# A two-layer hybrid decoder trunk: cross attention by token tile, first transfers reordered, DVE's low halves placed between evacuations, norms by Newton steps on DVE

## What is computed

```python
for l in range(2):
    h = rmsnorm(x, norm_mix[l])
    qa, ka, va, qb, kb, vb, qi, ki, wi, qc, kc, vc, g = split(h @ w_in[l])   # 5316 columns
    # three mixers: stick-breaking attention; top-64 sparse attention; sliding window attention
    merged = gates[0] * (o_a @ w_pa[l]) + gates[1] * (o_b @ w_pb[l]) + gates[2] * (o_c @ w_pc[l])
    x = x + merged @ w_out[l]
    # cross attention, 4 heads of 128, into 256 memory tokens
    q = rmsnorm(rmsnorm(x, norm_x[l]) @ w_xq[l], qn_x[l])
    k, v = split(rmsnorm(mem, norm_mem[l]) @ w_xkv[l]); k = rmsnorm(k, kn_x[l])
    x = x + softmax(q k^T / sqrt(128)) v @ w_xo[l]
    hf = rmsnorm(x, norm_ffn[l])
    x = x + (swiglu(hf) if l == 0 else top-2-of-8 expert swiglu(hf))
```

## Time and profile before

| | |
|---|---|
| median of 3 runs | 1813.37 us (1812.16 to 1819.61) |
| the profiled execution | 1814.6 us, span 1813.0 us |
| PE busy in the span | 95% |
| DVE, ACT, POOL busy | 78%, 61%, 5% |
| mean granted TensorE clock | 0.984 of full speed |

### The profile page before, as it was taken

The page is one execution under the profiler, slowest core; times in us unless marked ns, Lnnn a source line. Parts: engine busy times, 40 slices in busy tenths (PEclk is TensorE's granted clock), DMA queues, the critical chain, the costliest instruction groups (busy, mean ns, idle before and its releaser), DMA issues.

```text
span 1813.0 us, 22257 instructions
## 1 busy us (share of the span) xinstructions
PE 1717.1 (95%) x7776; PEld 1373.4 (76%) x7776; DVE 1405.6 (78%) x1258; ACT 1112.3 (61%) x1006; POOL 93.7 (5%) x68
## 2 busy tenths in 40 slices
PE   6999887999989998879999989999999999999999
PEld 5877666788768676667888878888788888788776
DVE  5798675554477967748888878888888888888897
ACT  4646354444345453537777777777777777877765
POOL 1200000000003000010000000000000000000440
PEclk9999998999999999979999999999999999999999
DMA  8533592555445325409999989999999999999985
GB/s 288 206 107 135 189 349 93 186 184 185 162 140 204 134 104 186 186 22 397 365 361 380 366 314 387 364 380 368 346 390 362 369 387 366 367 362 366 402 328 203
DMA packets 73791, 498.13 MB, mean 275 GB/s; under 512 B 8192, under 2 KB 8960, under 8 KB 17552
## 3 DMA queue, kind: packets, MB, share of 16 engines
q1 hardware_dynamic: 66000, 466.55, 67.9%
q0 software_dynamic: 7328, 29.87, 4.6%
q10 hardware_dynamic: 416, 1.08, 0.2%
HBM read 481.73 MB, written 15.73 MB: 274 GB/s over the span
## 4 chain that ended last, share of the span: by engine, by line
PE 77%; DVE 11%; ACT 4%; issue 3%; DVEq 3%; DMA 2%; ACTq 0%; SPq 0%; POOLq 0%
PE ps L516 24%; PE ps L520 24%; PE ps L512 24%; DVE w_lo L397 3%; DVE w_lo L901 1%; ACT w_hi L392 1%; PE ps L701 1%; DMA raw<-in_layer_tiles 1%; PE ps L1201 1%; DVE hT_lo L505 1%; DVE st L1447 1%; ACT w_hi L831 1%; DVEq L1450 1%; ACT scratch L1366 0%; DMA z<-rows_of_experts 0%
## 5 line engine op out<-in xcount | busy, mean ns | idle before, releaser
L512 PE MATMUL ps<-w_hi,hT_hi 128*128 128x512 f32 (+1 forms) x1552 | 436.5, 404 | 33.6 <-ACT hT_hi L500 10.6
L901 DVE TENSOR_TENSOR w_lo<-raw,w_hi 128x2048 fp32r<-128x2048 f32 x168 | 391.3, 2331 | 64.2 <-ACT w_hi L831 64.2
L901 DVE TENSOR_TENSOR w_lo<-z,w_hi 128x2048 fp32r<-128x2048 f32 x168 | 386.6, 2305 | 57.1 <-ACT w_hi L831 56.1
L516 PE MATMUL ps<-w_hi,hT_lo 128*128 128x512 f32 (+1 forms) x1552 | 424.3, 396 | 0.8 <-DVE hT_lo L505 0.4
L520 PE MATMUL ps<-w_lo,hT_hi 128*128 128x512 f32 (+1 forms) x1552 | 422.2, 394 | 0.7 <-DVE w_lo L397 0.7
L512 PEld LDWEIGHTS ps<-w_hi,hT_hi 128*128 128x128 f32 x1552 | 278.8, 190 | 96.7 <-ACT hT_hi L500 12.5
L516 PEld LDWEIGHTS ps<-w_hi,hT_lo 128*128 128x128 f32 x1552 | 290.9, 189 | 73.0 <-DVE hT_lo L505 4.1
L831 ACT ACTIVATE w_hi<-z 128x2048 fp32r<-128x2048 f32 x168 | 321.3, 1915 | 39.9 <-PE ps L520 36.2
L520 PEld LDWEIGHTS ps<-w_lo,hT_hi 128*128 128x128 f32 x1552 | 291.0, 189 | 71.2 <-DVE w_lo L397 1.6
L831 ACT ACTIVATE w_hi<-raw 128x2048 fp32r<-128x2048 f32 x168 | 321.1, 1912 | 25.5 <-PE ps L520 25.5
L397 DVE TENSOR_TENSOR w_lo<-raw,w_hi 128x2048 fp32r<-128x2048 f32 (+2 forms) x111 | 243.5, 2203 | 105.0 <-ACT w_hi L392 104.5
(11 more groups left out here) (260 smaller groups left out, 977.5 us busy)
## 6 DMA issues: line engine op xcount, KB each, us to landing
z<-in_moe_tiles SPq DMA_DIRECT2D x168, 1024.0 KB, 6.5
raw<-in_moe_tiles SPq DMA_DIRECT2D x168, 1024.0 KB, 6.5
raw<-in_layer_tiles SPq DMA_DIRECT2D x68, 1024.0 KB, 4.9
raw<-in_dense_tiles SPq DMA_DIRECT2D x33, 1024.0 KB, 4.8
rows_of_experts<-z POOLq DMA_DIRECT2D x1, 8704.0 KB, 37.8
raw<-in_layer_tiles SPq DMA_DIRECT2D x8, 512.0 KB, 3.6
z<-rows_of_experts POOLq DMA_DIRECT2D x8, 512.0 KB, 10.2
rows_of_experts<-z POOLq DMA_DIRECT2D x7, 512.0 KB, 8.1
```

What stands on the lines that cost most here:

```text
L512: pe.matmul(acc, hi[:, k, cols], wh, start=start and j == 0, stop=False)
L516: pe.matmul(acc, lo[:, k, cols], wh, start=False, stop=False)
L901: v.tensor_tensor(w_lo[:, ring, :], moe_raw(p), w_hi[:, ring, :].bitcast(F32), ALU.subtract) \
```

## The change

- **Cross attention** goes by token tile: both query slots for tile 0, then tile 1, with tile 0's query transposes between tile 1's two slots; ACT copies each tile's queries; the factor of each tile is made by itself; tile 0's probabilities are transposed and multiplied while tile 1's are being made; xo is worked tile by tile, with both column blocks in banks of their own.
- **Norms** (`dve_rsqrt`): an integer start value and three Newton steps, all on DVE, thirteen small instructions; no ACT function. The gains go into the split: ACT writes `hi` straight from PSUM by four instructions for each half with a per-partition scale, DVE subtracts by four `scalar_tensor_tensor`. The memory's low half moves from POOL to DVE.
- **Low halves**: in `dve_linear` and `dve_merge` one of the low halves is done after tile 0's evacuation, no longer ahead of it.
- **Merge**: the merged transposes wait for each half by itself.
- **First transfers**: SP issues the identity tile, the first half of x, slot 0, the second half of x, slots 1 and 2, the other constants, the memory.
- **Experts**: `dve_last` and its transposes go between the first two experts, the Exp to the start of the first; the last rows are loaded without waiting for the stores, and a small transfer behind the stores takes the place of that wait for the gathers.
- **Router**: the norm is finished ahead of the router's own work.

The core of the diff:

```diff
-            for _ in range(n):
+            for b in range(n):
+                if name == "xo":
+                    evacs.append([(by, counts[by] + 2 * i + b + 1) for i in range(TT)])
+                    counts[by] += TT * n * b
+                    continue
                 evacs.append([(by, counts[by] + i + 1) for i in range(TT)])
                 counts[by] += TT
...
+                cols = slice(h * NB, (h + 1) * NB)
+                sp.dma_start(x_sb[:, :, cols], t["x"][0].rearrange("(t p) d -> p t d", p=P)[:, :, cols]).then_inc(sem(f"x{h}_in"), 16)
+            sp.dma_start(ident, t["c_tiles"][0]).then_inc(sem("ident_in"), 16)
+            load_x(0)
...
+                    if s == 0:
+                        load_x(1)
                     if s == RING - 1:
+                        sp.dma_start(consts[:, 1:, :], t["c_tiles"][1:].rearrange("i p n -> p i n")).then_inc(sem("const_in"), 16)
                         load_memory(sp, 0)
...
             pool.wait_ge(sem("rows_T"), n_it)
+            load_rows(pool, n_it)
             pool.wait_ge(sem("rows_put"), n_it * 16)
-            load_rows(pool, n_it)
+            pool.dma_start(rows_all[0:1, 0:2], expert_rows[bass.ds(n_it * P - P, 1), 0:2]).then_inc(sem("rows_all"), 16)
...
             pool.tensor_tensor(bias[:, 0, 4:6, :], bias[:, 0, 4:6, :], bc(window.unsqueeze(1), [P, 2, 2 * P]), ALU.add)
             pool.tensor_tensor(bias[:, 1, :, :], bias[:, 1, :, :], bc(window.unsqueeze(1), [P, 6, 2 * P]), ALU.add)
             pool.drain().then_inc(sem("bias_ready"), 1)
-
-        def pool_memory_low(pool, l):
-            for i, ks in halves():
-                pool.wait_ge(sem("mem_H"), 2 * l + i + 1)
-                pool.tensor_tensor(o_lo[:, ks, :], memT[:, ks, :], o_hi[:, ks, :].bitcast(F32), ALU.subtract) \
...
-            act.activation(rstd[:, c], tmp[:, c], ACT.Exp, scale=-0.5).then_inc(sem("rs0"), 1)
-
-        def dve_var(v, name, width):
+            return {"mem": slice(30, 32), "xq0": slice(0, 4), "xq1": slice(4, 8)}.get(name) or slice(0, RS_N[name])
+
+        def dve_rsqrt(v, name, width, dst=None):
+
...
-
-            c, k = rs_cols(name), RS_AT[name, l]
-            v.wait_ge(sem("rs0"), k + 1)
-            v.tensor_tensor(tmp[:, c], rstd[:, c], rstd[:, c], ALU.mult)
-            v.drain()
-            v.tensor_tensor(tmp[:, c], tmp[:, c], var[:, c], ALU.mult)
-            v.drain()
-            v.tensor_scalar(tmp[:, c], tmp[:, c], -0.5, 1.5, ALU.mult, ALU.add)
-            v.drain()
-            return v.tensor_tensor(rstd[:, c] if dst is None else dst, rstd[:, c], tmp[:, c], ALU.mult)
+            v.tensor_scalar(var[:, c], ss[:, c], 1.0 / width, EPS, ALU.mult, ALU.add)
+            v.drain()
+            v.tensor_scalar(tmp[:, c].bitcast(I32), var[:, c].bitcast(I32), 1, None, ALU.logical_shift_right)
+            v.tensor_scalar(half[:, c], var[:, c], -0.5, None, ALU.mult)
+            v.drain()
+            v.tensor_scalar(rstd[:, c].bitcast(I32), tmp[:, c].bitcast(I32), -1, 0x5f3759df, ALU.mult, ALU.add)
+            for n in range(3):
+                v.drain()
+                v.tensor_tensor(tmp[:, c], rstd[:, c], rstd[:, c], ALU.mult)
+                v.drain()
+                v.tensor_tensor(tmp[:, c], tmp[:, c], half[:, c], ALU.mult)
+                v.drain()
+                ins = v.scalar_tensor_tensor(rstd[:, c] if dst is None or n < 2 else dst, tmp[:, c], 1.5, rstd[:, c],
+                                             ALU.add, ALU.mult)
+            return ins
...
-                v.wait_ge(sem(name + "_T"), 2 * l + i + 1)
-                g = gains[:, g0 + ks.start:g0 + ks.stop].unsqueeze(2)
-                v.tensor_tensor(dst[:, ks, :], psT[:, ks, :], bc(g, [P, KC // 2, S]), ALU.mult) \
-                    .then_inc(sem(name + "_F"), 1)
+                act.wait_ge(sem(name + "_T"), 2 * l + i + 1)
+                for k in range(ks.start, ks.stop):
+                    ins = act.activation(dst[:, k, :], psT[:, k, :], ACT.Copy, scale=gain_of(name, l, k))
+                ins.then_inc(sem(name + "_H"), 1)
+
+        def dve_lo_gain(v, name, l, hi, dst):
+            for i, ks in halves():
+                v.wait_ge(sem(name + "_H"), 2 * l + i + 1)
+                for k in range(ks.start, ks.stop):
+                    ins = v.scalar_tensor_tensor(dst[:, k, :], psT[:, k, :], gain_of(name, l, k), hi[:, k, :].bitcast(F32),
+                                                 ALU.mult, ALU.subtract)
+                ins.then_inc(sem(name + "_L"), 1)
...
                 last = s + (b + 1) * per - 1
-                ahead(dve_split_to, v, cnt, last, limit)
+                ahead(dve_split_to, v, cnt, last - 1, limit)
                 blk = blk0[name, l] + b
                 v.wait_ge(sem("tile0_done"), blk + 1)
                 take(b, 0).then_inc(sem("evac"), 1)
+                ahead(dve_split_to, v, cnt, last, limit)
                 v.wait_ge(sem("mm_done"), last + 1)
                 take(b, 1).then_inc(sem("evac"), 1)
...
-            for par in range(2):
-                pe_expert(pe, 0, par)
+            pe_expert(pe, 0, 0)
             pe.wait_ge(sem("last_hot"), 1)
             for i in range(TT):
                 ins = pe.transpose(ps[:, 7, i * P:(i + 1) * P], last_hot[:, i, :], ident)
             ins.then_inc(sem("last_T"), 1)
+            pe_expert(pe, 0, 1)
...
+                    act.wait_ge(sem("top_two"), 1)
+                    act.activation(g2[:, 0:2], g2[:, 0:2], ACT.Exp).then_inc(sem("gate_exp"), 1)
                 elif what == "y":
-                    if not (isinstance(ip, int) and ip == 0):
+                    if isinstance(ip, int):
+                        act.wait_ge(sem("last_T"), 1)
+                        act.activation(last_to_token, ps[:, 7, 0:2 * P], ACT.Copy).then_inc(sem("last_to_token"), 1)
+                    else:
                         act.wait_ge(sem("rows_put"), n * 16)
                     act_y(act, off + (MOE0 + 2))
...
+            dve_expert(v, 0, 0)
             dve_last(v)
+            dve_expert(v, 0, 1)
...
+        def pe_queries(pe, l):
+            s, blk = blocks["xq", l], blk0["xq", l]
+            for i in range(TT):
+                wait_evac(pe, blk - 1, i)
+                for h in range(2):
+                    x_lo = None
+                    if i == 0:
+                        pe.wait_ge(sem("x_H"), 2 * l + h + 1)
+                        x_lo = ("x_L", 2 * l + h + 1)
+                    ins = pe_tile_slot(pe, s + h, i, ps[:, LIN + i, :], 4 * h, h == 0, h == 1, x_lo)
+                    if i == 1:
+                        ins.then_inc(sem("mm_done"), 1)
+                        if h == 0:
+                            pe_query_T(pe, l, 0)
+                    elif h == 1:
+                        ins.then_inc(sem("tile0_done"), 1)
...
             pe.wait_ge(sem("x_kT"), l + 1)
+            pe_cross_scores(pe, l, 0)
+            pe_query_T(pe, l, 1)
+            pe_cross_scores(pe, l, 1)
+            pe_cross_probs_T(pe, l, 0)
+            pe.wait_ge(sem("x_pT_dve"), 2 * l + 1)
+            pe_cross_out(pe, l, 0, (0, 1))
+            pe_cross_probs_T(pe, l, 1)
+            pe_cross_out(pe, l, 0, (2, 3)).then_inc(sem("xo_T"), 1)
+            pe.wait_ge(sem("x_pT_dve"), 2 * l + 2)
+            pe.wait_ge(sem("x_pT_act"), l + 1)
+            pe_cross_out(pe, l, 1, (0, 1, 2, 3)).then_inc(sem("xo_T"), 1)
...
                 pe_turn(pe, "x", x_sb, blk=blk0["out", l])
                 pe_cross_keys(pe, l)
-                pe_linear(pe, "xq", l, h_ready="x")
+                pe_queries(pe, l)
                 pe_cross(pe, l)
-                pe.wait_ge(sem("xo_L"), 2 * l + 2)
-                pe_linear(pe, "xo", l)
+                pe_xo(pe, l)
                 pe_turn(pe, "ffn", x_sb, blk=blk0["xo", l])
                 if l == 0:
...
-                pe.wait_ge(sem("merged"), l + 1)
-                pe_turn(pe, "mrg", xn)
+                pe_turn(pe, "mrg", xn, halves_in=(("merged_half", l + 1), ("merged", l + 1)))
...
+        def act_cross(act, cnt, l):
+            for i in range(TT):
+                act.wait_ge(sem("x_queries_T"), 2 * l + i + 1)
+                c = slice(i * P, (i + 1) * P)
+                act.activation(headsT[:, 0:4, c], ps[:, i, :].rearrange("p (h s) -> p h s", h=4), ACT.Copy) \
+                    .then_inc(sem("x_qT"), 1)
+                act_split_to(act, cnt, end_of("xq", l) + 1 + i)
...
-                    dve_split_to(v, cnt, min(last + RING, lim))
                     blk = blk0[name, l] + b
                     for i in range(TT):
+                        dve_split_to(v, cnt, min(last + RING - 1 + i, lim))
...
-            ins.then_inc(sem("merged"), 1)
+                    if j == 2:
+                        ins.then_inc(sem(("merged_half", "merged")[b]), 1)
...
+            s, blk = blocks["xq", l], blk0["xq", l]
+            dve_split_to(v, cnt, s + 2)
+            for i in range(TT):
+                if i == 0:
```

(43 more changed lines are left out.)

247 lines of the change are left out of this document (110 added, 137 removed).

## The result

The changed kernel takes 1792.65 us (median of 4 runs, 1792.29 to 1796.7); the kernel before took 1814.01 on the same chip (4 runs, 1812.16 to 1819.61). The ratio is 0.988, 95% interval 0.9862 to 0.9899: faster by 1.2%. The profiled execution has a span of 1790.7 us, 22.3 less than before; 24.5 less were forecast.

A forecast was written before the change was run, and what follows sets the result against it. PE, busy 95%, was taken to bound the kernel, leaving its idle and low-clock time to win. Layer 0 -8.4, layer 1 -7.1 and experts -9.0 gave -24.5: 1814.6 to 1790.1, 1789 beside the median; range 1779 to 1802.

The forecast's parts named there:

- the signs named ahead: Traces: first product by 14 us, DVE-bound fourth in-projection block, 4 to 6 us probability waits, ranks 3 us later, among others.
- In projection: In projection start to fourth block: start 4.5 earlier, DVE's chain 5.7 longer in layer 0; net +1.1, layer 1 +0.3.
- Merge: Merge: new DVE order removes waits and pb's slow stretch (1.7), so the out projection starts 4.2 earlier a layer.
- The fallback of 2.5: Merge: if the clock still falls, the out projection starts only 2.5 earlier in place of 4.2.
- the first rival: Seams give back 13: merge clock 3.4, late slot 0 5, `dve_last` 1, cross attention 4; 1802, chance 0.2.
- Out: Out projection: ACT, freed of the root, has `w_hi` ready and one `w_lo` less precedes evacuation; 2.8 saved.
- Norms: Each norm: 13 small DVE operations, 3.0 us, 1.8 more on DVE; ACT loses 3.4 us of tables and functions.
- Cross attention: Cross attention by tile: first probabilities at +13.3 as before, PE idle 5, then halves overlap; 3.3 saved a layer.
- the cause named for the router: Router: root (3.0) and two 1.2 us multiplications precede the logits' copy on DVE, moving the gather back 2.9.
- Experts: Experts: wait for ACT at the second expert's end goes, -5.9; last rows -3.4; `dve_last` costs 0.3; together -9.0.
- the pipeline does nothing: Rival: cross attention gains 0, DVE bounds the rest, experts -6; only 5 faster, 1809, chance 0.11.
- The slower case: Rival: `w_lo` between evacuations blocks DVE on ACT's `w_hi` in 26 blocks, costing 49 us; 1839, chance 0.04.

The follow-up runs named there:

- the control: The changed kernel run again, unedited, beside other runs on the same chip: 1793.58 us, ratio 0.9877 to the kernel before.
- the two runs together: Changed kernel with memory's low half late, cross attention reordered, Exp table early, rows scaled on DVE: 1771.96 us with two Newton steps, 1777.39 with three.
- the two single ones: Changed kernel with only the memory's low half late, three Newton steps: 1787.5 us; the same with two Newton steps: 1778.24 us.

## Why the prediction was right, and where its terms were not

The forecast was faster, 1789 in 1779 to 1802; measured 1792.65. The sum is only 2.2 off the measured difference of spans because misses offset each other, which is luck in part: 4.3 of cost too little in the in projections, 1.6 of gain too little in the cross attentions and 2.0 in the experts. Single stages also move by 1.6 with nothing changed. The direction holds in every stage; the sizes of the in projection, the cross attention and the experts, and the part of the clock in the merge, were wrong. Of the signs named ahead, two were missed by little: the first product came at 14.52 and not by 14, and the wait for the first probabilities in layer 0 is 3.83 and not 4 to 6.

- **In projection, the largest miss: +1.1 and +0.3 forecast, +3.3 and +2.4 measured.** That DVE's chain becomes the bound is right: from the first high half of x (13.2) to the fourth block it is 45.8 against t + 45.2, and moving 3.2 of it away removed the wait. Part of that is luck: the second block came 18.2 after t, not 16.8, since DVE idled 1.55 between x's halves, and the rest of the chain was 0.8 shorter than counted. Two things were not in the sum. The gain at the start is 3.2 by the run with the old transfers, not 4.5: the landing of slot 0 was sized well (9.80 against 9.6), but PE's queue holds the transposes of x's second half ahead of the first product, and that half came at 12.90. And the wait of 3.34 is followed by four matmuls in 2.04 in place of 1.17 and more such, some 1.3 by the stage's end. In layer 1 the miss of 2.1 holds a clock step of 1.6 behind the second block (514 to 522, granted clock 0.75 and 0.82), which neither the kernel before nor the control has there; without it the stage is +0.8. The control has -0.8, as it also lacks the slow stretch behind the third gate block, which the kernel before has in layer 1 too. (The stage's terms, -4.5 and +5.7, give +1.2 and not +1.1.)
- **Merge: -4.2 forecast, -4.0 measured.** The cause is DVE's order, as forecast; undoing it costs 4.1 a layer (the share of the transposes in halves is not shown). The wait inside pb's second block (1.65 against 1.7) and pa's second block, 1.45 sooner against 1.4, came as counted. But the 1.7 put down to the slow stretch in pb were not the clock's: with the old order and full clock pc's first block comes just as late, 4.98 after pb's second. The fallback of 2.5 and the first rival's 3.4 rest on the same 1.7.
- **Out: -2.8 forecast, -2.6 and -2.3 measured, but the cause was half right.** I gave the gain to ACT, freed of the root, and to one `w_lo` less ahead of the evacuation. With ACT still free and the old order the wait is 2.19 again: the order alone decides it.
- **Norms.** 13 small operations came at 2.8 to 3.3 us, the longer ones with a gap of 0.4 to 0.5 inside, the shift and the integer arithmetic at 0.17 each like the others (3.1 for 30 columns). The first half of a turn took 1.55 on ACT and 1.66 on DVE, as taken. ACT is freed of two loads of 1.28 and two functions of 0.20, 3.0 a norm and not 3.4.
- **Cross attention: -3.3 forecast, -4.4 and -3.8 measured.** The first probabilities come 12.9 and 13.2 after the end of the queries, 13.3 forecast; the predicted wait of 5 is 3.83 and 4.87, behind one of 2.19 for tile 1's queries: these queries, tile 1's root and both maxima stand on DVE's chain. The two runs that reorder this chain bring the first probabilities 2.2 and 3.6 sooner after tile 0's query transposes, where 2.2 and 3.8 were expected. The gain beyond the forecast comes behind them: xo starts 9.4 and 9.6 after the first probabilities, 10.1 forecast.
- **x and queries, router:** 0.3 or less off. With the root late, the copy of the logits waits 2.23 in place of 5.01, as the cause named for the router says; the gather does not come sooner for it, since ACT's scaling needs the root.
- **Experts: -9.0 forecast, -11.0 measured.** The pair's end gave 6.9 (5.9 forecast), the last rows 3.7 (3.4), `dve_last` cost 0.2 (0.3). Not counted were 0.7 at each of two later places, which the run with the experts as before brings back, and 0.8 given back at a wait of 2.52 for a low half, behind two `w_lo` that took 7.28 together, elsewhere 4.49.

The rivals: the seams did give back, but at the in projection, not in the merge, for slot 0 or in the experts. That the pipeline does nothing is refuted by the stage itself. The slower case, DVE blocked on `w_hi` by the order between evacuations, shows nowhere: the changed kernel has no wait of PE for `w_hi` over 0.25, and the old order is the slower one by 16.2 in the plain projections and 8.2 in the merge. What stays open is what decides at which seam the clock falls, and why `w_lo` took longer at the last rows. With the clock, the worth of a third Newton step is known only roughly: 5.4 by the medians of the two runs together, 9.3 by those of the two single ones; by the spans of these it is 7.9, of which some 5.5 are left without the steps of the clock. No run takes back the cross attention by token tile, the Newton steps against ACT's Ln and Exp, the memory's low half on DVE or the early last rows: what these gave is read from landmarks of two traces, and their causes are argued.
